# Diagonal 16x16 blocks of the triangular inverses moved from TensorE to VectorE in a float32 model block on one core

## The reference, cut to what matters

```python
kk = jnp.einsum("bnhcd,bnhsd->bnhcs", k, k)
lower = jnp.where(strict, beta[..., :, None] * kk * decay, 0.0)
rhs = jnp.concatenate([v * beta[..., None], k * (beta * jnp.exp(g))[..., None]], axis=-1)
sol = lax.linalg.triangular_solve(lower, rhs, left_side=True, lower=True, unit_diagonal=True)
...
def step(S, inp):
    qk_i, qd_i, kd_i, u_i, w_i, gl_i = inp
    v_new = u_i - jnp.einsum("bhck,bhkv->bhcv", w_i, S)
    o = jnp.einsum("bhck,bhkv->bhcv", qd_i, S) + jnp.einsum("bhcs,bhsv->bhcv", qk_i, v_new)
    S = S * gl_i[..., None, None] + jnp.einsum("bhck,bhcv->bhkv", kd_i, v_new)
```

## Time and profile before

| | us |
|---|---|
| three executions: median (lowest to highest) | 1797.72 (1795.52 to 1797.75) |
| the profiled execution: its own time | 1797.27 |
| its span in the profile | 1795.1 |
| TensorE busy (matmul records) | 1711.0, 95% of the span |
| TensorE weight loads busy | 1370.9, 76% |
| VectorE, ScalarE, POOL busy | 877.8, 783.6, 202.0 |
| mean granted TensorE clock | 0.987 |

### The profile page before, as it was taken

The page is one execution under the profiler, slowest core; times in us unless marked ns, Lnnn a source line. Parts: engine busy times, 40 slices in busy tenths (PEclk is TensorE's granted clock), DMA queues, the critical chain, the costliest instruction groups (busy, mean ns, idle before and its releaser), DMA issues.

```text
span 1795.1 us, 21522 instructions
## 1 busy us (share of the span) xinstructions
PE 1711.0 (95%) x8308; PEld 1370.9 (76%) x8308; DVE 877.8 (49%) x1388; ACT 783.6 (44%) x1345; POOL 202.0 (11%) x233
## 2 busy tenths in 40 slices
PE   6799999999998899999999999999997999999998
PEld 4678888888877687777777778777675888888867
DVE  4746555555553535455545443544336532344336
ACT  3533544544543425555555532455544432333243
POOL 0111201211211200032222110000002000000011
...
GB/s 164 60 35 40 56 48 48 47 48 48 47 48 24 121 95 95 94 60 71 76 60 71 42 71 94 90 47 48 59 59 58 94 106 94 94 94 101 102 79 47
DMA packets 40164, 127.27 MB, mean 71 GB/s; under 512 B 4576, under 2 KB 9104, under 8 KB 40064
## 3 DMA queue, kind: packets, MB, share of 16 engines
...
q10 hardware_dynamic: 912, 0.99, 0.2%
...
## 4 chain that ended last, share of the span: by engine, by line
PE 89%; DVE 4%; ACT 3%; issue 2%; POOL 1%; DMA 0%; SPq 0%; ACTq 0%; DVEq 0%
PE ps L637 87%; PE ps L968 1%; DVE wl L1706 1%; PE ps L783 1%; DVE qkv L1742 1%; POOL h L2402 1%; ACT wh L1119 1%; DMA wraw<-in_wa 0%; DVE mo L2278 0%; ACT xr L1383 0%; DVE U L2019 0%; DVE xm L2269 0%; ACT xm L1651 0%; POOL L L2387 0%; DVE sqa L2077 0%
## 5 line engine op out<-in xcount | busy, mean ns | idle before, releaser
L637 PE MATMUL ps<-xr,wh 128*128 128x512 f32 x2752 | 922.1, 416 | 15.7 <-DVE wl L1706 14.3
L637 PEld LDWEIGHTS ps<-xr,wh 128*128 128x128 f32 x2752 | 501.4, 190 | 141.8 <-issue 42.8
L637 PE MATMUL ps<-xr,wl 128*128 128x512 f32 x1376 | 542.1, 394 | 0.0
L1706 DVE TENSOR_TENSOR wl<-wraw,wh 128x1024 fp32r<-128x1024 f32 x214 | 261.8, 1238 | 152.5 <-ACT wh L1119 151.3
L637 PEld LDWEIGHTS ps<-xr,wl 128*128 128x128 f32 x1376 | 260.2, 189 | 57.0
L1119 ACT ACTIVATE wh<-wraw 128x1024 fp32r<-128x1024 f32 x214 | 220.3, 1047 | 20.1 <-PE ps L637 17.8
L637 PE MATMUL ps<-xm,wh 128*128 128x512 f32 x640 | 203.7, 400 | 9.9 <-DVE xm L2271 7.0
L637 PEld LDWEIGHTS ps<-xm,wh 128*128 128x128 f32 x640 | 122.5, 193 | 40.9 <-issue 9.1
L637 PE MATMUL ps<-xm,wl 128*128 128x512 f32 x320 | 126.9, 397 | 0.0
L2387 POOL TENSOR_SCALAR L<-L,m 128x256 f32<-128x256 f32 (+1 forms) x128 | 76.1, 614 | 349.1 <-DVE m L2170 349.1
L2331 POOL TENSOR_TENSOR Mm<-AT,masks 128x512 f32<-128x512 f32 x56 | 82.8, 1485 | 239.3 <-PE ps L637 122.9
...
## 6 DMA issues: line engine op xcount, KB each, us to landing
...
```

What stands on the lines that cost most here:

```text
L637: return e.matmul(out, w, x, start=start, stop=stop, skip_group_check=True)
L1706: e.tensor_tensor(m.wl[:, i % N_SPLIT, :], m.raw[:, i % N_RAW, :], m.wh[:, i % N_SPLIT, :].bitcast(F), ALU.subtract).then_inc(s.wlo, 1)
```

## The change

The four smallest doublings (to 16x16 blocks) leave TensorE. POOL makes one mask m16 out of the masks 0 to 3 and the identity at the start, and multiplies AT by it (D, into Mm[1]). VectorE sums the eight column blocks of D away (dc: 128 partitions, 4 chunks, 16 columns). SyncE moves dc with four transfers so that each of the 32 blocks of a head lies in one partition (bn), VectorE inverts all 32 at once with 17 instructions on 32 partitions (`invert`), SyncE moves the result back with four transfers (uc), and VectorE spreads it over U. T after levels 3 and 4 is made by VectorE's 32x32 transposes, T after level 5 by a transpose on TensorE that ScalarE drains. Levels 4, 5 and 6 stay on TensorE as P and U products, in calls 8 to 14; call 15 makes wT. The calls 8 to 15 stand in rounds 20 to 27; 14 to 19 are empty for prep on TensorE. On VectorE dc stands in round 11, the three parts of `invert` in 13, 14 and 15, and U3 and T3 in 19. On SyncE, which had no prep, the two sets of transfers stand in rounds 12 and 17. The working tiles lie in tiles that are not in use then.

```diff
@@ -422,6 +423,10 @@
+        self.m16 = self.masks[:, 0, :]
+        self.dc, self.uc = a.new([4, 16], name="dc"), a.new([4, 16], name="uc")
+        self.bu = self.masks[:, 2:4, :].rearrange("p a b -> p (a b)")
+        self.bn, self.by, self.bp = self.XF[:, 31, 0:256], self.XF[:, 31, 256:320], self.XF[:, 30, :]
...
@@ -565,14 +573,14 @@
-PREP_P = 27
+PREP_P = 16
-    ("silu0", "silu1", "sq0", "sq1", "silu2", "silu3", "eb", "ln0", "ex0", "ln1", "ex1", "E", "v0", "v1", "T",
-     "P1", "P2", "P3", "P4", "P5", "P6", "w"))}
+    ("silu0", "silu1", "sq0", "sq1", "silu2", "silu3", "eb", "ln0", "ex0", "ln1", "ex1", "E", "v0", "v1", "P4",
+     "P5", "T5", "P6", "w"))}
-    ("dv", "y0", "y1", "qdn", "at", "qk", "kg", "kd", "U0", "T1", "U1", "T2", "U2", "T3", "U3", "T4", "U4", "T5", "U5",
-     "U6"))}
-PREP_O = {n: i + 1 for i, n in enumerate(("sel", "M0", "M1", "M2", "M3", "M4", "M5", "M6"))}
+    ("dv", "y0", "y1", "qdn", "at", "qk", "dc", "kg", "kd", "U3", "T3", "U4", "T4", "U5", "U6"))}
+N_INV = 17
+PREP_O = {n: i + 1 for i, n in enumerate(("sel", "D", "M4", "M5", "M6"))}
...
@@ -811,33 +819,29 @@
             e.wait_ge(s.prep_a, prep_a(h, f"silu{2 + j}"))
             end(6 + j, turn4(o, lambda n: v[:, ch[n]]), (s.prep_a, prep_a(h, f"v{j}")))
             yield
-        o = begin(8)
-        e.wait_ge(s.prep_v, prep_v(h, "U0"))
-        end(8, turn4(o, lambda n: U[:, n, :]), (s.prep_a, prep_a(h, "T")))
-        yield
-        call = 9
-        for i in range(1, 7):
+        yield from idle(6)
+        call = 8
+        for i in range(4, 7):
             o = begin(call)
-            if i == 1:
-                e.wait_ge(s.prep_a, prep_a(h, "T"))
+            if i == 6:
+                e.wait_ge(s.prep_a, prep_a(h, "T5"))
             else:
                 e.wait_ge(s.prep_v, prep_v(h, f"T{i - 1}"))
             e.wait_ge(s.prep_o, prep_o(h, f"M{i}"))
             end(call, four(o, lambda n: m.Mm[:, i % 2, n, :], lambda n: m.Tm[:, n, :]), (s.prep_a, prep_a(h, f"P{i}")))
             call += 1
             yield
-            if i < 6:
-                o = begin(call)
-                e.wait_ge(s.prep_a, prep_a(h, f"P{i}"))
-                e.wait_ge(s.prep_v, prep_v(h, f"U{i - 1}"))
-                end(call, four(o, lambda n: U[:, n, :], lambda n: m.Pm[:, n, :]), (s.prep_v, prep_v(h, f"T{i}")))
-                call += 1
             o = begin(call)
             e.wait_ge(s.prep_a, prep_a(h, f"P{i}"))
-            e.wait_ge(s.prep_v, prep_v(h, f"U{i - 1}"))
             end(call, four(o, lambda n: m.Pm[:, n, :], lambda n: U[:, n, :]), (s.prep_v, prep_v(h, f"U{i}")))
             call += 1
             yield
+            if i == 5:
+                o = begin(call)
+                e.wait_ge(s.prep_v, prep_v(h, "U5"))
+                end(call, turn4(o, lambda n: U[:, n, :]), (s.prep_a, prep_a(h, "T5")))
+                call += 1
+                yield
         o = begin(call)
         e.wait_ge(s.prep_v, prep_v(h, "U6"))
         end(call, four(o, lambda n: m.kg[:, n, :], lambda n: U[:, n, :]), (s.prep_a, prep_a(h, "w")))
@@ -1320,23 +1324,22 @@
                 e.wait_ge(s.rec_p, REC_P * (h - 2) + 11)
             did(e.activation(m.vt[:, par, :, j * 128:(j + 1) * 128], o, ACT.Copy))
             yield
-        o = product(8)[1]
-        if h:
-            e.wait_ge(s.prep_p, prep_p(h - 1, 24))
-        did(e.activation(m.Tm[:], o, ACT.Copy))
-        yield
-        call = 9
-        for i in range(1, 7):
+        yield from idle(6)
+        for call, i in ((8, 4), (10, 5), (13, 6)):
             o = product(call)[1]
-            if i > 1:
-                e.wait_ge(s.prep_p, prep_p(h, call - 1))
+            if i > 4:
+                e.wait_ge(s.prep_p, prep_p(h, 9 if i == 5 else 11))
             elif h:
-                e.wait_ge(s.prep_p, prep_p(h - 1, 25))
+                e.wait_ge(s.prep_p, prep_p(h - 1, 14))
             did(e.activation(m.Pm[:], o, ACT.Copy))
             yield
             yield
-            call += 3 if i < 6 else 2
-        o = product(call)[1]
+            if i == 5:
+                o = product(12)[1]
+                e.wait_ge(s.prep_p, prep_p(h, 10))
+                did(e.activation(m.Tm[:], o, ACT.Copy))
+                yield
+        o = product(15)[1]
         if h >= 2:
             e.wait_ge(s.rec_p, REC_P * (h - 2) + 11)
         did(e.activation(m.wT[:, par], o, ACT.Copy))
@@ -1991,33 +1994,107 @@
         yield
         did(e.tensor_tensor(m.qkT[:, par], product(4), m.Dm[:], ALU.mult))
         yield
+        e.wait_ge(s.prep_o, prep_o(h, "D"))
+        if h:
+            e.wait_ge(s.bin, 64 * h)
+        did(e.tensor_reduce(m.dc[:], m.Mm[:, 1].rearrange("p n (b c) -> p n c b", b=8), AX.X, ALU.add))
         o = product(5)
         if h:
-            e.wait_ge(s.prep_p, prep_p(h - 1, 26))
+            e.wait_ge(s.prep_p, prep_p(h - 1, 15))
         if h == 0:
             e.wait_ge(s.gate_v, 12)
             e.wait_ge(s.gate_a, 11)
         did(e.tensor_tensor(m.kg[:], o, bc(m.egn[:, col]), ALU.mult))
         did(e.tensor_tensor(m.kd[:, par], o, bc(m.ekd[:, col]), ALU.mult))
-        e.wait_ge(s.prep_o, prep_o(h, "M0"))
-        did(e.tensor_tensor(U, m.ident.unsqueeze(1).to_broadcast([128, 4, 128]), m.Mm[:, 0], ALU.subtract))
-        yield
-        yield from idle(3)
-        call = 9
-        for i in range(1, 7):
-            yield
-            call += 1
-            if i < 6:
-                o = product(call)
-                e.wait_ge(s.prep_a, prep_a(h, "T"))
-                if i > 1:
-                    after(f"T{i - 1}")
-                did(e.tensor_tensor(m.Tm[:], m.Tm[:], o, ALU.subtract))
-                call += 1
+        yield
+        yield
+        yield from invert(h)
+        yield
+        yield
+        e.wait_ge(s.bout, 64 * (h + 1))
+        if h == 0:
+            e.wait_ge(s.m16, 4)
+        free_of_recurrence()
+        did(e.tensor_tensor(U.rearrange("p n (b c) -> p n b c", b=8), m.uc[:].unsqueeze(2).to_broadcast([128, 4, 8, 16]),
+                            m.m16.rearrange("p (b c) -> p b c", b=8).unsqueeze(1).to_broadcast([128, 4, 8, 16]),
+                            ALU.mult))
+        after("U3")
+        if h:
+            e.wait_ge(s.prep_p, prep_p(h - 1, 13))
+        did(e.transpose(m.Tm[:].rearrange("p n c -> p (n c)"), U.rearrange("p n c -> p (n c)")))
+        yield
+        for call, i in ((9, 4), (11, 5), (14, 6)):
+            yield
             o = product(call)
             after(f"U{i - 1}")
             did(e.tensor_tensor(U, U, o, ALU.subtract))
-            call += 1
+            if i == 4:
+                after("U4")
+                did(e.transpose(m.Tm[:].rearrange("p n c -> p (n c)"), U.rearrange("p n c -> p (n c)")))
+            yield
+            if i == 5:
+                yield
+        yield
+
+    def invert(h):
+
+
+        done = [N_INV * h]
+
+        def did(ins):
+            ins.then_inc(s.inv, 1)
+            done[0] += 1
+
+        def last():
+            e.wait_ge(s.inv, done[0])
+
+        def at(t, i, j, *dims):
+            v = t[0:32, :]
+            return bass.AP(v.tensor, v.offset + 16 * i + j, [list(v.ap[0])] + [list(x) for x in dims])
+
+        def cat(t, o, *dims):
+            v = t[0:32, :]
+            return bass.AP(v.tensor, v.offset + o, [list(v.ap[0])] + [list(x) for x in dims])
+
+        N, V, Y, P = m.bn, m.bu, m.by, m.bp
+        if h:
+            e.wait_ge(s.bout, 64 * h)
+        else:
+            e.wait_ge(s.unit, 2)
+        e.wait_ge(s.bin, 64 * (h + 1))
+
+        did(e.tensor_scalar(at(V, 0, 1, (34, 8)), at(N, 0, 1, (34, 8)), -1.0, None, ALU.mult))
+        last()
+
+        did(e.tensor_tensor(cat(Y, 0, (2, 4), (1, 2)), at(N, 0, 2, (68, 4), (16, 2)), at(V, 2, 3, (68, 4), (0, 2)), ALU.mult))
+        last()
+        did(e.tensor_tensor(at(N, 0, 3, (68, 4), (16, 2)), at(N, 0, 3, (68, 4), (16, 2)), cat(Y, 0, (2, 4), (1, 2)), ALU.add))
+        last()
+        did(e.tensor_tensor(cat(Y, 0, (2, 4), (1, 2)), at(N, 1, 2, (68, 4), (1, 2)), at(V, 0, 1, (68, 4), (0, 2)), ALU.mult))
+        did(e.tensor_scalar(at(V, 1, 2, (68, 4), (1, 2)), at(N, 1, 2, (68, 4), (1, 2)), -1.0, None, ALU.mult))
+        last()
+        did(e.scalar_tensor_tensor(out=at(V, 0, 2, (68, 4), (1, 2)), in0=at(N, 0, 2, (68, 4), (1, 2)), scalar=-1.0,
+                                   in1=cat(Y, 0, (2, 4), (1, 2)), op0=ALU.mult, op1=ALU.subtract))
+        yield
+        for b in (4, 8):
+            n = 8 // b
+            last()
+            for i in range(n):
+                r = 2 * b * i
+                did(e.tensor_tensor(cat(P, b ** 3 * i, (b * b, b), (b, b), (1, b)), at(N, r, r + b, (16, b), (0, b), (1, b)),
+                                    at(V, r + b, r + b, (0, b), (1, b), (16, b)), ALU.mult))
+            last()
+            did(e.tensor_reduce(cat(Y, 0, (1, n * b * b)), cat(P, 0, (b, n * b * b), (1, b)), AX.X, ALU.add))
+            last()
+            for i in range(n):
```

(69 more changed lines are left out.)

10 lines of the change are left out of this document (6 added, 4 removed).

## The result

The changed kernel takes 1832.1 us (1829.4 to 1833.2) against 1797.3 (1795.5 to 1797.8) of the kernel before on the same chip: ratio 1.0193, 95% interval 1.0176 to 1.0211. The profiled execution took 1832.65 us with a span of 1830.8. The sign is the forecast's; the size is 35 us where it said 21.

The account below looks back on a forecast made before the run. TensorE's instruction stream was taken as the bound; heads 1 to 6 add 14.4, head 0 3.4 and head 7 3.1, 20.9 us more on 1797.27, giving 1818. Forecast range 1804 to 1833; wider range 1783 to 1846.

Parts of the forecast that it names:

- the sum: Over the whole kernel: 14.4 for heads 1 to 6, 3.4 for head 0, 3.1 for head 7, 20.9 us more.
- The second wait: TensorE in front of call 8, heads 1 to 6: waits for T3, 5.5 us more.
- step 8: Clock after TensorE's two waits: the first's slowdown is swallowed by the second; 1.3 us a head, between 0 and 1.7.
- The chain is short: Rival, transfers and invert in eight heads: at least 2.6 us less a head than 9.6; 1794 or 1784; 20%.
- The cover holds: Rival: squares don't hang on cin, or rounds 14 to 19 are long enough; 78 us come in full, 1719; 7%.
- The chain is long: Rival: transfers over few partitions, issues 1 us or more, or strided reductions double; 4 us more a head, 1850; 15%.

Follow-up runs that it names:

- e12: Changed kernel plus unused matmuls in heads 1 to 6, six before the channel sum at the recurrence's end and three before call 8: 1830.3 us.
- e2: Changed kernel without the four transfers that bring the inverted blocks back, for all heads, with uc set to zero once: 1829.0 us.
- e11: Changed kernel; first transfers ahead of weight load, large part of invert behind cin, half-width unused matmuls before call 8, in heads 0 and 7 before later calls: 1779.9 us.
- e3: Changed kernel with SyncE's first set of transfers issued in round 11, ahead of the weight load, in place of round 12: 1815.2 us.

## Why the prediction was right, and where its size was off

**The condition.** It held as put: a call that goes is worth its length only if its place isn't filled with a wait. The calls did go (TensorE's busy sum fell) and the chain filled their place. The sum fell by 42.6 us and the time rose by 35. The Trainium skill ("Trainium Kernel Development and Optimization", Performance Expectations) calls matmul busy time a bad metric for the distance to roofline, because matmuls are pipelined; the trace agrees for the calls that went (0.89 us from start to start, 1.06 by busy time), while the rise in time has another reason, the waits and the clock.

**Step by step, head 4 (the prediction's head 3), on its time before** (measured less 15.76). dc ran at 334.05 (forecast 334.2), but for 1.04 us and not 0.69. The transfers issue from 338.0 (forecast 337.6) and VectorE resumes at 342.1 (341.8). The fourth transfer was issued at 340.1 and VectorE went on 2.0 us later, where the sum had 2.4. The Trainium skill ("DMA: Bandwidth & Descriptors", Anatomy of one DMA) gives about 2.0 us, for transfers that GpSimd issues; these are SyncE's, and they took as long. The 3 us that the sum would have been lower by it did not come: the fourth was issued 0.6 us later than forecast, after a first that was 0.4 late and with 0.65 to 0.72 us from one issue to the next, not 0.60. `invert` took 6.14 us and not 5.4: the 13 short instructions 2.66 (2.6), the four long ones 3.48 (2.8), because the products on 32 partitions took 1.02 and 1.06 us. The channel sum waited 5.91 us (5.1) for the squares, queued as forecast behind cin. Call 8 started at 359.6 (359.2). That it came so close owes something to luck: xreg took 1.29 us for two instructions and not 1.99, which made up for `invert`. The second wait was 2.6 us and not 5.5, because TensorE spent the rest on its slow channel sum and projections; e12 showed that this is the same time under another name, as step 8 had it ("swallowed by the second").

**Middle heads.** 2.5 us each for heads 1 to 5, forecast 2.4, and part of this agreement is luck. Where no call is slow (heads 1, 2 and 5) the loss is 1.8 to 2.1 us, forecast 1.1 without the clock: 0.4 or so more in front of call 8 (30.0 to 30.2 us after AT, forecast 29.6) and 0.4 behind it (14.2, forecast 13.8). The clock was forecast at 1.3 us in every head; it cost 1.0 to 1.2 behind call 8 in heads 3 and 4, 0.4 on average. So the waits and calls were priced too low and the clock in these heads too high. Head 6 lost 4.4 us, and the 2.0 more are the clock too: 1.1 from call 8 to call 15 (15.2 us, not 14.2) and 1.1 from there to AT 7 (27.9 us at a granted clock of 0.88). In e2, whose head 6 lost 2.0 us, the same two stretches are 14.2 and 26.8 us, the latter at 0.94 as in the kernel before.

**The term that was mis-sized** is the clock in heads 0 and 7, 1.3 us each. For it I took the loss behind one wait of the earlier trace rows, as if TensorE came back to full speed after it. In head 7 call 8 was even earlier against AT than forecast (22.1 us, not 23.7), but from its start to that of call 15 the granted clock was 0.50, that is 1.2 GHz, and it and all calls behind it took 2.05 us. With some time at either side of them:

```profile
570.00:602.00 32.00, 15.86 (x61) 13.66 (x62) 9.60 (x14) 6.21 (x9) 1.26 (x1) 0.54 0.01 2
```

19.76 - 13.44 = 6.3 us in the calls (e11 has them at full clock) and 1232.1 - 1228.4 = 3.7 behind them, 10 in place of 1.3. In head 0 call 8 came at 101.8, near the forecast (100.6, and 0.7 for the later start; the 86.9 in its sum leaves out 0.5 of dc, with which it is 101.8); from there to call 15 took 16.3 us where the forecast has 13.2 and e11 14.3. Together with what follows, head 0 cost 7.6 and not 3.4. These two terms and head 6 are 4.2 + 7.5 + 2.0 of the 14.8 us by which the span rose more than the 20.9 of the sum. A thin chain stood there before too, at a granted clock of 1.00 with calls of 1.05 to 1.13 us; there a level had three calls on TensorE, and now it has two, behind a wait of 9.5 us. Which of the two lets the clock fall was not separated.

**The rivals.** "The chain is short" put its turning point at 2.6 us a head between SyncE's release and the end of `invert`. e3 took 2.9 us out of it (4.54 to 1.66), and call 8 came 3.0 us earlier after AT (27.1 and not 30.0). The period of heads 1 to 5 fell by 2.9 us each, and the time by 17, to 1815. So the rival's mechanism is real and its price per head right; but the load stands in front of the transfers in six heads, not eight, and the clock loss that was to go with the waits stayed (calls of 2.05 us in head 1 of e3 as well). "The cover holds" had nothing for it. "The chain is long" was right in its rows (reductions of 512 elements 1.04 us for dc, products with strides 1.02 to 1.06) but those were 1 us a head, not 4.

**Open:** what decides at which call the clock falls, since the same instructions gave 16.3 and 18.0 us in head 0; whether the wait filled whole would be enough in head 7; and whether e11's counts are the best ones.
